# One schedule table and one order of work changed in a transformer kernel: the second token group's ticks, and ScalarE's place for them in a slot

## What is computed

```python
hn = modulate(rmsnorm(x, norm1_g), shift1, scale1)
qa, ka, va, qi, ki, wi, qb, kb, vb, ga, gb = split(hn @ w_in)
ya = dsa_attention(qa, ka, va, qi, ki, wi, rel_bias)    # each query keeps its 128 best keys, chosen by an index score
yb = stick_breaking_attention(qb, kb, vb)               # weight = exp(log_sigmoid(z) + suffix sums of log(1 - sigmoid))
x = x + gate1 * ((sigmoid(ga) * (ya @ w_proj_a) + sigmoid(gb) * (yb @ w_proj_b)) @ w_out)
hn2 = modulate(rmsnorm(x, norm2_g), shift2, scale2)
x = x + gate2 * peer_ffn(hn2, peer_wq, sub_keys, u, v)  # per token 8 heads x 16 experts of 16384: rows of u and v
x = rmsnorm(x, final_g)
# then a second block: forgetting attention with 16 meta tokens, pooled means, gated feed-forward
```

## Time and profile before

| | |
|---|---|
| median of the runs | 2427.18 us |
| profiled execution | 2421.59 us, of it the span 2419.9 us |
| TensorE busy | 1974.6 us (82%) |
| VectorE busy | 1397.5 us (58%) |
| ScalarE busy | 1069.9 us (44%) |
| GpSimd busy | 567.8 us (23%) |
| gathers of expert rows | 512, 543.30 MB of 758.52 MB moved |
| weight tiles through the ring | 340, 512 KB each |

### The profile page before, as it was taken

The page is one execution under the profiler, slowest core; times in us unless marked ns, Lnnn a source line. Parts: engine busy times, 40 slices in busy tenths (PEclk is TensorE's granted clock), DMA queues, the critical chain, the costliest instruction groups (busy, mean ns, idle before and its releaser), DMA issues.

```text
span 2419.9 us, 41177 instructions
## 1 busy us (share of the span) xinstructions
PE 1974.6 (82%) x16172; PEld 1358.4 (56%) x16172; DVE 1397.5 (58%) x3264; ACT 1069.9 (44%) x2529; POOL 567.8 (23%) x541
## 2 busy tenths in 40 slices
PE   5888896888776769887845798988888885999999
PEld 4777784555444536554502453345666553677887
DVE  6654767574577456666577767666555543223554
ACT  3334554444553452234333567844444322343443
POOL 0000003231223223333334334343333331000000
PEclk8999998998878889998956896688999997999999
DMA  9822449997679779999999999999999996313554
GB/s 344 328 105 96 153 155 395 364 346 276 244 276 377 264 292 409 417 418 418 417 421 420 407 412 402 386 404 418 417 417 417 418 418 273 115 53 108 188 181 167
DMA packets 140497, 758.52 MB, mean 313 GB/s; under 512 B 16224, under 2 KB 22496, under 8 KB 74384
## 3 DMA queue, kind: packets, MB, share of 16 engines
q0 software_dynamic: 74784, 543.30, 55.5%
q1 hardware_dynamic: 60864, 208.23, 23.3%
q10 hardware_dynamic: 4656, 4.36, 0.5%
HBM read 751.60 MB, written 4.23 MB: 312 GB/s over the span
## 4 chain that ended last, share of the span: by engine, by line
PE 42%; DMA 28%; DVE 12%; ACT 10%; issue 4%; POOL 2%; ACTq 0%; SPq 0%; DVEq 0%; another core or an unknown queue 0%
DMA arena<-experts,eidx 25%; DVE arena L2472 6%; PE psum L1320 6%; PE psum L1167 4%; PE psum L837 4%; PE psum L838 4%; PE psum L839 4%; DMA ring<-w_stream 3%; POOL arena L2449 2%; PE psum L1444 2%; PE psum L1617 2%; PE psum L1494 2%; DVE ring_low L2492 2%; PE psum L1148 2%; ACT arena L2093 1%
## 5 line engine op out<-in xcount | busy, mean ns | idle before, releaser
L2472 DVE CUSTOM_DVE_ANT_0 arena<-arena 128x1024 f32<-128x1024 f32 (+3 forms) x592 | 690.6, 1183 | 373.2 <-DMA arena<-experts,eidx 337.6
L2449 POOL DMA_INDIRECT arena<-experts,eidx x512 | 558.9, 1092 | 1304.0 <-PE psum L1320 1026.4
L1320 PE MATMUL psum<-arena,sq 32*32 32x512 f32 x8192 | 373.9, 717 | 268.6 <-ACT sq L2101 232.1
L2087 ACT ACTIVATE arena<-arena 128x2 f32<-128x2 f32 x256 | 52.0, 203 | 679.8 <-DVE arena L2472 647.2
L1320 PEld LDWEIGHTS psum<-arena,sq 32*32 32x32 f32 x8192 | 81.6, 110 | 404.0 <-ACT sq L2101 304.2
L1167 PE MATMUL psum<-arena,ring 128*128 128x256 f32 x976 | 241.8, 404 | 17.7 <-ACT arena L1941 17.7
L1167 PEld LDWEIGHTS psum<-arena,ring 128*128 128x128 f32 x976 | 193.7, 203 | 76.8 <-ACT arena L1941 25.5
L1639 PE MATMUL psum<-arena,ring 128*128 128x256 f32 x704 | 163.5, 387 | 1.2 <-DVE arena L2469 1.2
L837 PE MATMUL psum<-hn_high,w_high 128*128 128x256 f32 (+1 forms) x416 | 127.2, 306 | 44.2 <-DVE ring_low L2492 21.7
L1639 PEld LDWEIGHTS psum<-arena,ring 128*128 128x128 f32 x704 | 131.8, 192 | 50.1 <-issue 31.8
L2101 ACT ACTIVATE sq<-sq,arena 128x32 f32<-128x32 f32 x512 | 136.8, 314 | 25.2 <-ACT arena L2093 1.9
(11 more groups left out here) (379 smaller groups left out, 3406.3 us busy)
## 6 DMA issues: line engine op xcount, KB each, us to landing
ring<-w_stream SPq DMA_DIRECT2D x340, 512.0 KB
arena<-w_ada SPq DMA_DIRECT2D x48, 512.0 KB, 6.9
arena<-experts,eidx POOLq DMA_INDIRECT x512
arena<-cum_rows POOLq DMA_DIRECT2D x1, 2112.0 KB, 9.9
x<-xT SPq DMA_DIRECT2D x2, 1024.0 KB, 8.3
arena<-rel_rows ACTq DMA_DIRECT2D x4, 512.0 KB, 13.0
arena<-rel_rows POOLq DMA_DIRECT2D x1, 1024.0 KB, 10.3
k_early<-arena POOLq DMA_DIRECT2D x2, 512.0 KB, 7.7
```

The costliest lines, as they stand in the source:

```text
L1320: last = mm(bank(4 + 2 * odd + a)[QUART * b:QUART * b + QUART, :], diag[k, s, :], rows[k, s, D + a * 512:D + (a + 1) * 512], start=c == 0, ...
L2087: steps(op(pre[:, s:s + 2], pre[:, s:s + 2], ACT.Gelu))
L2449: nc.gpsimd.indirect_dma_start(rows[:, s, :], None, experts, bass.IndirectOffsetOnAxis(ap=eidx[:, n // P % 2, n % P:n % P + 1], axis=0)).t ...
L2472: return V.tensor_tensor_reduce(out=out, in0=a, in1=b, scale=1.0, scalar=0.0 if op1 == ALU.add else -TAKEN, op0=op0, op1=op1, accum_out=accum)
```

## The change

The late block has 285 ticks in place of 251. `late_ticks` gives two ticks in every eighth slot from slot 0 on (before: from slot 128 on), and all three compute engines take the ticks by the same function. By this the late attention's steps lie over more slots: stick-breaking heads have 8 ticks each (before 6), steps of the chosen-key attention 6 (before 4), dense tiles of the attentions stand 3 ticks apart (before 2). Where one engine's step uses another's result, the distance between their ticks is changed, mostly to 3 or more where ScalarE's result is used. In ScalarE's slot the order was: diagonals, exponentials of the best experts (L1851), first group's queries and keys with `high`, ticks; it now is: exponentials, queries, keys with `high`, ticks, diagonals. ScalarE's `early_query` stands in slot 4j (before 4j + 2), `early_keys` in 4j + 2 (before 4j + 3). The index scores' relu has 4 buffers (before 2). The ring's order follows the new slots.

```diff
-L_MEAN, L_ROOT, L_KI, L_WI, L_QI, L_IDX = 1, 6, 10, 14, 18, 21
-L_TOP = 39
-L_B, L_BH = 42, 6
-L_A, L_AS = 100, 4
-L_G, L_GM = 138, 6
+L_MEAN, L_ROOT, L_KI, L_WI, L_QI, L_IDX = 3, 6, 14, 16, 18, 22
+L_TOP = 41
+L_B, L_BH = 44, 8
+L_A, L_AS = 113, 6
+L_G, L_GM = 169, 6
...
-           + [(L_B - 8 + 2 * L_BH * p + 2 * j, (KB + p, QB + p, S_V + HP + p)[j]) for p in range(HP) for j in range(3)]
-           + [(L_A - 6 + 2 * L_AS * q + 2 * j, (KA + q, QA + q, S_V + q)[j]) for q in range(HP) for j in range(3)])
+           + [(L_B - 9 + 2 * L_BH * p + 3 * j, (KB + p, QB + p, S_V + HP + p)[j]) for p in range(HP) for j in range(3)]
+           + [(L_A - 9 + 2 * L_AS * q + 3 * j, (KA + q, QA + q, S_V + q)[j]) for q in range(HP) for j in range(3)])
...
+def late_ticks(n):
+    return 1 + (n % 8 == 0) if n < 2 * P else 0
+SLOT_OF = [n for n in range(2 * P) for _ in range(late_ticks(n))]
...
-def late_ticks(n):
-    return 1 + (n >= P and n % 8 == 0)
...
 TensorE
-                    for shift, f in ((6, late_weighted), (3, late_sums), (0, late_z)):
+                    for shift, f in ((9, late_weighted), (6, late_sums), (0, late_z)):
-                    for shift, f in ((8, late_values), (6, late_transposes), (0, late_scores)):
+                    for shift, f in ((13, late_values), (9, late_transposes), (0, late_scores)):
-                    j = due(t, L_Q + 3, 2, 2 * PH)
+                    j = due(t, L_Q + 4, 2, 2 * PH)
 ScalarE
-                    n = LATE_TILE.get(t - 2)
+                    n = LATE_TILE.get(t - 1)
-                    h = due(t, L_B + 5, L_BH, NH)
+                    h = due(t, L_B + 6, L_BH, NH)
                     if h is not None:
                         late_weights(h)
-                    for shift, f in ((7, late_turned), (5, late_normalize), (3, late_exponents)):
+                    for shift, f in ((10, late_turned), (5, late_normalize), (2, late_exponents)):
             for n in range(HEADS * PK):
-                if n % 2 == 0:
-                    diagonals(n)
                 for choice, p in PLAN[n]:
                     if p == BEST_PART:
                         best_weights(choice)
+                j = due(n, 0, 4, 2 * PH - LEAD)
+                if j is not None:
+                    early_query(LEAD + j)
                 j = due(n, 2, 4, 2 * PH - LEAD)
                 if j is not None:
-                    early_query(LEAD + j)
+                    early_keys(LEAD + j)
                     if j < 2 * PH - LEAD - 2:
                         high(S_WQ + LEAD + 2 + j)
...
+                for _ in range(late_ticks(n)):
+                    next(late, None)
+                if n % 2 == 0:
+                    diagonals(n)
 VectorE
-                    h = due(t, L_B + 2, L_BH, NH)
+                    h = due(t, L_B + 4, L_BH, NH)
                     if h is not None:
                         late_softplus(h)
-                    st = due(t, L_A + 4, L_AS, 2 * HP)
+                    st = due(t, L_A + 5, L_AS, 2 * HP)
                     if st is not None:
                         late_shares(st)
-                    m = due(t, L_O + 3, 2, KT)
+                    m = due(t, L_O + 1, 2, KT)
                     if m is not None:
                         late_out(m)
```

More of the change, by code:

```diff
@@ L82, in turn_at @@
     return TURN0 if j == 0 else P * (j + 1) + 6
+def late_ticks(n):
+    return 1 + (n % 8 == 0) if n < 2 * P else 0
+SLOT_OF = [n for n in range(2 * P) for _ in range(late_ticks(n))]
+assert len(SLOT_OF) >= L_END
 def ring_order():
-    queries = [(4 * (j - LEAD), 0, S_WQ + j) for j in range(LEAD, 2 * PH)]
-    both = sorted(queries + [(t, 1, tile) for t, tile in L_DENSE])
-    return [(0, tile) for tile in range(S_WQ + LEAD)] + [(g, tile) for _, g, tile in both]
+    queries = [(4 * (j - LEAD), -1, 0, S_WQ + j) for j in range(LEAD, 2 * PH)]
+    both = sorted(queries + [(SLOT_OF[t], t, 1, tile) for t, tile in L_DENSE])
+    return [(0, tile) for tile in range(S_WQ + LEAD)] + [(g, tile) for _, _, g, tile in both]
 RING_ORDER = ring_order()
@@ L105, in late_bank @@
     if S_OUT <= tile < S_WQ:
-        return 1 + (tile - S_OUT) % 3
+        return 1 + (tile - S_OUT + 1) % 3
     if tile >= S_WQ:
@@ L1276, in late_keys @@
                 late_emptied(pe, "dense", S_WQ + j)
-                claim(3, "key", 16 + j)
-                fill(key_products(j, 3, j), 3, "key", 16 + j)
+                b = 3 * (j % 2)
+                claim(b, "key", 16 + j)
+                fill(key_products(j, b, j), b, "key", 16 + j)
             def late_block():
@@ L1674, in _ @@
                         turn(j, (n - turn_at(j)) // 8)
-                for _ in range(late_ticks(n) if n < PAIR else 0):
+                for _ in range(late_ticks(n)):
                     next(late, None)
@@ L1945, in late_relu_of @@
                 late_filled(act, "idx", n)
-                act.wait_ge(l_relu_used.sem, l_relu_used.free(n, 2))
-                emptied(op(late_relu[:, n % 2, 0:w], bank(2 + n % 2, w), ACT.Relu), "idx", n)
+                act.wait_ge(l_relu_used.sem, l_relu_used.free(n, 4))
+                emptied(op(late_relu[:, n % 4, 0:w], bank(2 + n % 2, w), ACT.Relu), "idx", n)
             def late_loads(u):
@@ L2030, in late_block @@
                             op(n1[:, k, :], x[:, k, META + PAIR:], ACT.Square).then_inc(l_squared.sem, 1)
-                    if t in (L_ROOT, L_N2 + 1):
+                    if t in (L_ROOT, L_N2):
                         late_root(int(t > L_ROOT))
-                    for c, first in enumerate((L_ROOT + 2, L_N2 + 3)):
+                    for c, first in enumerate((L_ROOT + 4, L_N2 + 4)):
                         half_of = due(t, first, 1, 2)
@@ L2074, in late_block @@
                         op(n1[:, k, :], x[:, k, META + PAIR:], ACT.Square).then_inc(l_squared.sem, 1)
-                    j = due(t, L_Q + 4, 2, 2 * PH)
+                    j = due(t, L_Q + 5, 2, 2 * PH)
                     if j is not None:
@@ L2388, in _ @@
                     sum_out(n // P - 1)
-                for _ in range(late_ticks(n) if n < PAIR else 0):
-                    next(late, None)
                 for _ in range(pair_ticks(n)):
@@ L2858, in late_block @@
                 for t in range(L_END):
-                    for c, first in enumerate((L_ROOT + 1, L_N2 + 2)):
+                    for c, first in enumerate((L_ROOT + 3, L_N2 + 3)):
                         half_of = due(t, first, 1, 2)
```

44 lines of the change are left out of this document (21 added, 23 removed).

## The result

The changed kernel takes 2468.0 us (median of 4 runs, 2462.3 to 2469.4) against 2425.8 (4 runs, 2421.1 to 2431.8) of the kernel before on the same chip: 1.0168 times as long, interval 1.014 to 1.0196. Forecast were 2417 us. The profiled execution took 2468.13 us, span 2466.4.

A forecast was written before the change was run, and what follows sets the result against it. Transfers at 418 GB/s bound most of the kernel; in slots 0 to 135 a chain through TensorE and ScalarE loses 134 us. +17 - 6 - 27 + 6 = -10 us, from the median 2427.18 to 2417; range 2380 to 2450.

The forecast's parts named there:

- Slots 0 to 39: Start of the expert stage: 28 us for `high` plus 11 for copies less 22 saved, +17 us; bounds -10, +34.
- the sum's own 11 us for the copies: Slots 4j at the start: query's copy ahead of the diagonals costs six times 1.9 us, 11 us.
- The copies: Start: TensorE's waits for ScalarE's query copy (17.7 us) and keys copy (4.2) go, -22 us.
- `high`: Start: `high`, ahead of its slot's diagonals, waits for ring tiles: 28 us in all, 9 of them at slot 14.
- Rival 1: Ring's wait decides: `high` waits at six or more slots, holding `combine`; +34 at the start, +20 in all, 2447; chance 0.20.
- Its own sign: Mark for the ring's wait deciding: waits that end in diagonals among slots 8 to 34 exceed some 45 us.
- Slots 40 to 99: Stick-breaking heads: 56 us of waits go, 55 come; -6 us taken; bounds -25, +15.
- Slots 100 to 149: Chosen-key attention: 160 us in place of 187, -27 us; bounds -41 and 0.
- 4 us exposed in five of eight steps: Chosen-key attention: after the scores, masks, exponentials and diagonals leave TensorE waiting 4 us in five of eight steps: 21 us.
- Slots 150 to 511: Transfers at 418 GB/s hide small waits; queries' part adds 18 us against about 8 spare: +6 us; bounds 0, +20.
- the marks that I had set: Expected in the table by stretches and waits: slower start, heads about 240 us, attention 160 us, 418 GB/s from slot 150.
- Rival 4: Attention tiles still share bank 1, so pauses stay and the attention gains nothing: +17 us, 2444; chance 0.05.

The follow-up runs named there:

- experiment 9: Kernel of experiment 8 with the first group's query and keys copies back in slots 4j+2 and 4j+3, still ahead of ticks and diagonals: 2448.02 us, 1.0089.
- experiment 8: Changed kernel with ScalarE's relu of an index product back to one tick behind its product: 2473.29 us, 1.0174.
- experiment 10: The combination: kernel before with heads eight ticks apart, attention four as before, evacuation one tick behind, relu in its product's tick, old ScalarE order and start ticks: 2366.59 us.
- (11): Kernel of experiment 10 with the relu of an index product one tick behind its product: 2349.6 us, 0.9682.
- (12): Kernel of experiment 7 with the relu one tick earlier, in its product's own tick, diagonals ahead of it: 2384.25 us, 0.982.
- (2): Changed kernel with only `high` moved behind the diagonals of its slot: 2454.3 us, 1.0126.
- (6): Changed kernel with the start ticks of before, ScalarE's new order kept: 2468.0 us, 1.0189.
- (5): Kernel of experiment 1 with the second group's ticks up to slot 40 as before and later steps two ticks earlier: 2374.09 us, 0.9787.
- (1): Changed kernel with its new ticks but ScalarE's old order within a slot (diagonals, copies, ticks last): 2387.96 us, 0.9882.
- experiment 7: Kernel before with one line changed, dense tiles evacuated one tick behind instead of two: 2375.3 us, 0.9785.

## Why the prediction was wrong

The profiled executions differ by 46.5 us, forecast were -10. I go by the sum's own terms; 2 us lie ahead of slot 0.

**Slots 0 to 39: +17 forecast, +55 measured, over the bound of +34. This step failed.** The bound itself had left out the sum's own 11 us for the copies (56 + 11 - 22 is 45), but 55 is over that too. One term had the wrong sign, one was missing, TensorE's busy time was taken as unchanged, and one term was too large.
- *The copies.* "What goes: TensorE's waits for ScalarE's copy": they did go, all 22 us. But the copies wait for TensorE ahead of the diagonals (38.0 and 13.0 us in the rows above), and taking them back to their slots won 12 us (experiment 9). -11 was forecast, +12 is measured.
- *The relu* was not in the sum at all. One tick earlier means in the tick of its own product: +12 in the changed kernel (8), +16 in the combination (11), +7 in the kernel with the old ticks (12). I had listed what waits for evacuations, not what the relu itself waits for.
- *The clock.* I counted waits and kept TensorE's busy time. The granted clock fell from 0.89 to 0.75, between its levels of 1.2 and 2.4 GHz, and the same products took 26 us more, half of the excess. In slots 0 to 7 (371 to 406 us) it was already 0.74; there TensorE had paused 6.2, 1.9, 2.0 and 5.0 us ahead of four `combine`s in a row. This half is not a fourth cause beside the others: most of what experiments 8 and 9 win is this busy time.
- *`high`* was forecast at 28 us and measured at 16 (2). The wait of 9 us at slot 14 was 10.7; besides it `high` found its tile landed nearly everywhere (10.8 us of waiting in all, 2 times), and the other waits that were ascribed to it stay without it. Rival 1 had the right sign and the time closest to the result (2447), but the wrong mechanism: without its wait the kernel still takes 2454. Its own sign, over 45 us of waits in slots 8 to 34, didn't come either: they are 38.

16 + 12 + 12 make 40 of the 55 us, if they add, which was not tried in one kernel. The start ticks cost 20 us in the new order (6) and 2 in the old (5), so the parts don't simply add; how the rest divides stays open. In the old order the relu alone accounts for the start's excess: 162 and 160 us in experiments 5 and 10, 144 with the relu one tick later (11), 146 before.

**Slots 40 to 99: -6 forecast, -8 measured.** Busy time is 187 us as before. The sum had 55 us of waits and took 6 off by judgement; measured inside the stretch are 47, against 55 before. That the order pays back what the new ticks win held in the main: the ticks take 33 us off (1), the order puts 25 back. That the number came out so close is in part luck: by its own waits the sum would have been -1.

**Slots 100 to 149: -27 forecast, -7 measured.** The stretch went from 195 to 180 us, of which 7.5 are the six gate tiles that moved behind. TensorE's busy time is 113.6 us for 113 forecast; the waits are 66 for 40. "4 us exposed in five of eight steps" is the term that was mis-sized: there are 17 waits of 3.9 us on average, at two of three `combine`s. And the sum never asked what the evacuation would give alone: experiment 7 has 154 us here with the old distances, near the transfers' 153. The new distances didn't win anything in this stretch: experiment 1 takes 168 us with the old order, although six gate tiles have left it.

**Slots 150 to 511: +6 forecast, +12 measured, of which 8 are the moved tiles.** The forecast had taken these tiles out of the time to compare for slots 100 to 149, so without them it is +4 for +6. 11 of the 12 us lie in slots 150 to 255, 1 behind them. (By the forecast's own terms, 18 us against spare time of about 8, it should have been +10.)

38 us of the miss lie in the start and 20 in the attention. Of the marks that I had set, four came true (start over 138 us, no wait of a tile for its evacuation, 235 us for the heads, waits near 3 and 5 us there), three not: `combine` waits of 4 to 9 us in slots 10, 14, 18, 22 and 30, of which slot 30 alone fits (5.0); 160 us at over 380 GB/s, where it is 180 at 329; 418 from slot 150, where it is 414. Rival 4 fell with the earlier trace rows answered: those waits are gone although bank 1 is still alone. The Trainium skill's "Perfetto Trace Analysis", section "Identifying Performance Opportunities", says that consistent bubbles can mean too few buffers; here experiment 7 removed these waits with the same single bank, by one line of order that gave 50 us. The Trainium skill's 2.66 us for a table switch ("ScalarE: Activation LUTs", section "What ACT_TABLE_LOAD costs") isn't borne out by the timeline of experiment 10 either: the load starts at 481.58, right behind the last diagonal, takes 1.28 us, and the next activation starts 1.29 us after the load did.

## What to carry to other kernels

Where engines work in order, it paid here to let an instruction that waits for a product stand one tick behind it, neither in its tick (the relu) nor two behind (the evacuation), and not ahead of what another engine needs next. When you move one, ask of each instruction in its tick both who waits for it and what it waits for. Change one thing at a time: here the new ticks together were worth 1.2% and the new order cost more than that, while one part of the ticks, the evacuation one tick sooner, was worth 2.2% alone. The rest of the ticks thus cost more than it gave. Against experiment 7, experiment 1 wins 31 us in the heads and loses 17 in the start, 14 in the attention and 8 behind it, where the moved tiles went. Where TensorE is busy for 80% of a stretch, price each new pause with the clock too, since here half of the start's loss was the same products at a lower clock.

## What the runs showed of the hardware that was not expected

A loss of clock can cost as much as the added waits themselves. The kernel before had 27 us of idle time in slots 0 to 39 at a clock of 0.89; the changed one has 56 at 0.75, and TensorE's busy time rose by 26 us beside 29 of idle time.

Neither the sum of the pauses nor their number foretells the clock of a stretch. Experiment 9 has 50 us of idle time in slots 0 to 39, nearly as much as the changed kernel's 56, and 20 waits for its 19, but a clock of 0.83 in place of 0.75. In experiment 7 the heads have 14 us less of idle time than before, and the clock is 0.82 in place of 0.85. The clock switches between its two levels within these stretches; which pauses make it fall was not found.

The 26 us by which single executions differ ahead of slot 0 go with the clock as well. The stretch from 180 to 240 us of a long execution (2488.24 us, experiment 8):

```profile
180.00:240.00 60.00, 57.56 (x220) 40.07 (x219) 15.12 (x46) 14.43 (x35) 0.00 (x0) 0.57 0.03 9
```

The same stretch of the changed kernel's execution:

```profile
180.00:240.00 60.00, 52.06 (x348) 42.32 (x348) 27.24 (x74) 24.59 (x62) 0.00 (x0) 0.94 0.23 77
```

The code there is the same, the clock is 0.57 against 0.94, and 220 products are done in place of 348, with TensorE busy for 57.6 of 60 us in the long one; slot 0's `combine` starts at 397.8 us in place of 371.2. The fifth experiment's profiled execution shows 0.57 there too. What decides between the two was not found; every median of few runs carries it as an uncertainty of up to 26 us, and only the stretches tell a change of 10 us from it.
